# Row maxima of attention: the negated maxima reach row 96 of the query tile by DMA between SBUF tiles

## The reference, cut to what matters

```python
def attend(q, keys, vals, scale):
    s = jnp.einsum('bqhgd,bkhd->bhgqk', q, keys) * scale
    p = jax.nn.softmax(s.astype(jnp.float32), axis=-1).astype(vals.dtype)
    return jnp.einsum('bhgqk,bkhe->bqhge', p, vals)
...
    keys = jnp.concatenate([k_c, k], axis=1)
    vals = jnp.concatenate([v_c, v], axis=1)
```

## Time and profile before

| what | value |
|---|---|
| time, median of 3 runs | 1147.48 us (1145.49 to 1149.68) |
| span of the profiled execution (it has no time of its own beside it) | 1146.1 us |
| TensorE matmuls busy | 1072.0 us, 94% of the span |
| VectorE, ScalarE, GpSimd busy | 440.2, 368.3 and 127.5 us |
| mean granted clock of TensorE | 0.974 |
| heads of layer 0, first to last score product | about 363 to 583 us |
| heads of layer 1 | about 914 to 1088 us |

### The profile page before, as it was taken

How to read it: one execution, slowest core, us unless ns; L and a number is a source line. 1 busy time by engine, 2 the same in 40 slices (tenths; PEclk the granted TensorE clock), 3 DMA queues, 4 the chain that set the end, 5 groups by cost and what they waited for, 6 DMA issues and landing times.

```text
span 1146.1 us, 11426 instructions
## 1 busy us (share of the span) xinstructions
PE 1072.0 (94%) x4139; PEld 610.6 (53%) x4139; DVE 440.2 (38%) x797; ACT 368.3 (32%) x690; POOL 127.5 (11%) x148
## 2 busy tenths in 40 slices
PE   2799999999999999999899899999998999999996
PEld 0455555655455544455568655555444544445474
DVE  1342103312473433554453433122237444454453
ACT  3322113100113344566650332112001234455712
POOL 2000000000242001000440200000003300100530
PEclk8899999999999999999999899999998899999998
DMA  9801012201200222122022411120222000003021
GB/s 351 288 1 56 2 54 74 74 19 56 74 1 1 74 74 77 71 74 74 1 111 69 145 51 55 55 73 1 74 75 73 1 1 1 0 29 119 1 93 73
DMA packets 50965, 74.29 MB, mean 65 GB/s; under 512 B 7812, under 2 KB 30688, under 8 KB 50784
## 3 DMA queue, kind: packets, MB, share of 16 engines
q1 hardware_dynamic: 47088, 60.81, 15.8%
q0 software_dynamic: 3824, 12.77, 3.0%
HBM read 69.37 MB, written 4.19 MB: 64 GB/s over the span
## 4 chain that ended last, share of the span: by engine, by line
PE 86%; DVE 4%; issue 3%; ACT 3%; DMA 2%; POOL 1%; SPq 1%; ACTq 0%; POOLq 0%; DVEq 0%
PE bank L1329 30%; PE pv L1497 10%; PE bank L1548 6%; PE bank L1320 5%; PE bank L1457 3%; PE bank L1579 3%; PE bank L1581 3%; PE bank L1580 3%; PE bank L1435 3%; PE bank L1466 3%; PE bank L1425 2%; DMA W<-in_w_mod 2%; PE bank L1273 2%; PE bank L1405 2%; PE bank L1474 2%
## 5 line engine op out<-in xcount | busy, mean ns | idle before, releaser
L1329 PE MATMUL bank<-hA,W 128*128 128x512 f32 (+1 forms) x992 | 348.3, 510 | 2.7 <-DVE hA L882 1.5
L1329 PEld LDWEIGHTS bank<-hA,W 128*128 128x128 f32 x992 | 187.8, 190 | 154.3 <-issue 142.4
L771 ACT ACTIVATE hA<-bank 128x512 f32<-128x512 f32 (+1 forms) x168 | 93.1, 563 | 91.9 <-PE bank L1548 64.0
L1127 DVE TENSOR_REDUCE mxp<-bank 128x1 f32<-128x384 f32 x192 | 96.5, 551 | 51.0 <-PE bank L1457 50.8
L1497 PE MATMUL pv<-hA,vg 128*128 128x512 f32 (+1 forms) x168 | 85.1, 588 | 6.7 <-ACT hA L771 6.4
L1497 PE MATMUL pv<-hA,XA 128*128 128x512 f32 (+1 forms) x168 | 82.1, 570 | 1.5 <-ACT hA L771 1.5
L1548 PE MATMUL bank<-hA 97*128 97x512 f32 (+1 forms) x168 | 78.1, 565 | 0.0
L1145 DVE SCALAR_TENSOR_TENSOR hA<-pv,hA 64x512 f32<-64x512 f32 (+1 forms) x36 | 21.6, 600 | 113.5 <-ACT hA L714 113.3
L1320 PE MATMUL bank<-W,hA 128*128 128x384 f32 x192 | 63.7, 486 | 0.0
L1580 PE MATMUL bank<-W_parts,hA_parts 128*128 128x512 f32 x160 | 62.3, 389 | 0.0
L911 DVE SCALAR_TENSOR_TENSOR YA<-tz,bank 128x512 f32<-128x512 f32 (+1 forms) x24 | 14.4, 599 | 108.3 <-ACT tz L573 108.3
(11 more groups left out here) (209 smaller groups left out, 1467.9 us busy)
## 6 DMA issues: line engine op xcount, KB each, us to landing
W<-in_w_mod SPq DMA_DIRECT2D x12, 2048.0 KB, 8.0
W<-in_w_in SPq DMA_DIRECT2D x6, 1536.0 KB, 8.5
W<-in_w_in SPq DMA_DIRECT2D x8, 1024.0 KB, 6.1
W<-in_w_out SPq DMA_DIRECT2D x4, 2048.0 KB, 7.8
W<-in_w_in SPq DMA_DIRECT2D x8, 512.0 KB, 4.3
XA<-in_x SPq DMA_DIRECT2D x4, 512.0 KB, 10.9
XA<-in_x POOLq DMA_DIRECT2D x4, 512.0 KB, 7.4
x_between_layers<-XA POOLq DMA_DIRECT2D x4, 512.0 KB, 2.9
```

The lines of the kernel that those rows point to most:

```text
L771: act.activation(prob[slot % 4][:, 0:nq], ps("sc", l, h, q0, kt)[:, 0:nq], ACT.Exp, scale=MLA_SCALE if h < MLA_H else GQA_SCALE)\
L1127: dve.tensor_reduce(mxp[:, t, half:half + 1], ps("mx", l, h, q0, t, half)[:, 0:384], AX, ALU.max).then_inc(*up("part_max", l, h, q0, t, half))
L1329: mm = pe.matmul(p[:, 0:c[1]], w[:, k, s * P:s * P + P], hT[:, k, c[0]:sum(c)], start=(k == 0), stop=(k == KD - 1))
```

## The change

The products of `max_rows` and the copies of `neg_max` are gone. SP moves each column of `nmx` into its 128 columns of row 96 by a DMA: for each head 6 DMAs of 128 words in layer 0 and 4 in layer 1, all from one queue, after the wait for `neg_max`. SP's stream is reordered for this: the first two blocks after the `w_in` blocks are issued ahead of head 0's rows, the others one by one behind the rows of the heads that carry modulation. TensorE waits for all rows of a head (`nm_row`) before its first unit. `MAX_FROM` goes from (3, 2) to (2, 1), so the next head's maxima products start a unit earlier; the new `MOD_AT` keeps the modulation in its units. VectorE's wait before a column of `nmx` is written again now names the rows of head h - 2.

```diff
--- before.py
+++ after.py
@@ -83,7 +83,8 @@
         **{f"z{i}": (4 + i // 4, i % 4) for i in range(8)}}
 LAST_OF = ["ckv0", "gq2", "glak", "tok5", "z3", "z7"]
 RING = 6
-MAX_FROM = (3, 2)
+MAX_FROM = (2, 1)
+MOD_AT = (1, 0)
 
 
 def chunks_of(name, layer):
@@ -358,8 +359,30 @@
             for i in range(1, 4):
                 block_dma(i)
             sp.dma_start(con[:, P:C_END], a["consts"][:, P:C_END]).then_inc(*dma("con_in"))
-            for i in range(4, len(W_SEQ)):
-                block_dma(i)
+
+            def neg_max_row(l, h):
+
+                sp.wait_ge(*at("neg_max", l, h))
+                if h >= 2:
+                    sp.wait_ge(*at("filled", "sc", l, h - 2, 256, TILES - 1))
+                lat, b = lat_of(l), h % 2
+                row = qh[b][96:97, lat] if h < MLA_H else q_high[b][96:97, lat].bitcast(F32)
+                for t in range(TILES - lat.start // P):
+                    with nc.allow_non_contiguous_dma("one word of each partition"):
+                        sp.dma_start(row[:, P * t:P * t + P], nmx[:, b, lat.start // P + t:lat.start // P + t + 1])\
+                            .then_inc(*dma("nm_row", l, h))
+
+            for l in range(DEPTH):
+                for b in range(6):
+                    block_dma(W_POS[("in", l, b)])
+                turns = [h for h in heads if mod_of_head(l, h)]
+                after = W_POS[("in", l, 5)] + 1
+                for i in range(2):
+                    block_dma(after + i)
+                for h in heads:
+                    neg_max_row(l, h)
+                    if h in turns:
+                        block_dma(after + 2 + turns.index(h))
 
 
         @block.gpsimd
@@ -738,21 +761,12 @@
                         act.activation(y_hi[:, k, lat_of(l)], Y[:, k, lat_of(l)], ACT.Copy)\
                             .then_inc(*up("y_hi", l, k))
 
-                def neg_max(h):
-                    for q0, nq, nk in qbs(l):
-                        act.wait_ge(*at("filled", "nm", l, h, q0))
-                        queries = (qh if h < MLA_H else q_high)[h % 2]
-                        act.activation(queries[96:97, q0:q0 + nq], ps("nm", l, h, q0)[96:97, 0:nq], ACT.Copy)\
-                            .then_inc(*up("nm_row", l, h, q0))
-                        let_go(("nm", l, h, q0), "nm_row", l, h, q0)
-
                 head_in(0)
                 round_q(0)
                 for t in out_tiles(l):
                     o_out(t)
                 slot = 0
                 recips = [] if l == 0 else [(0, heads[-1], 256)]
-                neg_max(0)
                 for h in heads:
                     todo = [(q0, nq, kt) for q0, nq, nk in qbs(l) for kt in range(nk // P)]
                     more = h + 1 < len(heads)
@@ -780,9 +794,9 @@
                         if j < 2 and more and h + 1 >= MLA_H:
                             gqa_in(h + 1, j + 1)
                         m = mod_of_head(l, h)
-                        if m and m[2] < 4 and j == MAX_FROM[l] - 2:
+                        if m and m[2] < 4 and j == MOD_AT[l]:
                             mod_rows(*m[1:])
-                        if m and m[2] >= 4 and j == MAX_FROM[l] + 1:
+                        if m and m[2] >= 4 and j == MOD_AT[l] + 3:
 
                             act.wait_ge(*at("filled", "vp", l, TILES - 1))
                             act.wait_ge(*at("filled", "kp", l, MLA_H - 1, LAT))
@@ -799,8 +813,6 @@
                             w_high(2 * c // KD, (2 * c % KD, 2 * c % KD + 1))
                         if j == 3 and len(qbs(l)) == 2:
                             recip(h, *qbs(l)[0][:2])
-                    if more:
-                        neg_max(h + 1)
 
                 y_high((2, 3))
                 recip(heads[-1], *qbs(l)[-1][:2])
@@ -1109,9 +1121,9 @@
 
                 def maxima(h):
                     if h >= 2:
-                        dve.wait_ge(*at("filled", "nm", l, h - 2, 256))
+                        dve.wait_ge(*at("nm_row", l, h - 2))
                     elif l:
-                        dve.wait_ge(*at("filled", "nm", l - 1, 10 + h, 256))
+                        dve.wait_ge(*at("nm_row", l - 1, 10 + h))
                     for q0, nq, nk in qbs(l):
                         for t in range(q0 // P, (q0 + nq) // P):
                             if q0 == 0:
@@ -1457,16 +1469,6 @@
                         close(pe.matmul(p[:, 0:n], q[:, t * P:t * P + P], k[:, n * half:n * half + n],
                                         start=True, stop=True), "mx", l, h, q0, t, half)
 
-                def max_rows(h):
-                    pe.wait_ge(*at("neg_max", l, h))
-                    for q0, nq, nk in qbs(l):
-                        p = open_("nm", l, h, q0)
-                        for j in range(nq // P):
-                            t = q0 // P + j
-                            mm = pe.matmul(p[96:97, P * j:P * j + P], nmx[:, h % 2, t:t + 1], ident, start=True,
-                                           stop=True)
-                        close(mm, "nm", l, h, q0)
-
                 def values(tiles):
                     for t in tiles:
                         p = open_("vp", l, t)
@@ -1528,14 +1530,13 @@
                     else:
                         groups = []
                     flush(1)
-                    max_rows(h)
                     if h + 1 < len(heads):
                         project_k(h + 1)
                     flush(0)
                     units = [(q0, nq, kt, nk // P) for q0, nq, nk in qbs(l) for kt in range(nk // P)]
                     for j, (q0, nq, kt, nkt) in enumerate(units):
                         if kt == 0:
-                            pe.wait_ge(*at("nm_row", l, h, q0))
+                            pe.wait_ge(*at("nm_row", l, h))
                             pe.wait_ge(*at("kh_ones", l, 1))
                             if h >= MLA_H:
                                 pe.wait_ge(*at("q_both", l, h))
@@ -1558,9 +1559,9 @@
                         slot[0] += 1
 
                         m = mod_of_head(l, h)
-                        if m and j == MAX_FROM[l] - 2:
+                        if m and j == MOD_AT[l]:
                             mod(*m[1:])
-                        if m and j == MAX_FROM[l] + (-1 if m[2] < 4 else 1):
+                        if m and j == MOD_AT[l] + (1 if m[2] < 4 else 3):
                             mod_turn(*m[1:])
                         flush(2)
                         if j >= MAX_FROM[l]:
```

## The result

The changed kernel takes 1194.13 us (median of 4 runs, 1191.21 to 1194.83) and the kernel before 1147.59 us in its 4 runs on the same chip. The ratio is 1.0405, with a 95% interval of 1.0385 to 1.0424: the change costs 46.5 us. The direction was forecast; the size was not. 1194 us lies outside the range, beyond every rival.

What follows compares the result with a forecast made beforehand. TensorE, with 86% of the last-ending chain, was taken to set the heads' pace. Terms -11.8 + 5.7 + 11.5 + 9.6 + 2 = +17 us on 1147.5 us gave 1164 us (rounded down), range 1142 to 1184 us.

Steps and rivals of the forecast that it cites:

- The removed work: Boundaries into MLA heads 0 to 4: removed products count in full, 5 x 1.40 + 5 x 0.96 = 11.8 us saved.
- In layer 0 ... nothing there waits: MLA heads, layer 0: context units and modulation product stand ahead, so the earlier maxima products cause no wait.
- each such head grows by 1.72 us: Layer 1 MLA heads: early maxima products wait for rounded queries; +5.2 us for heads 1 to 3, +0.5 in head 0.
- L: Time from the end of the negated maxima to the row in the query tile: 4.3 us layer 0, 3.5 layer 1.
- The clock: TensorE's granted clock falls after new stalls: +2 us in all, bounds 0 and 24 us.
- Most of the slow stretch falls where the head waits for ScalarE anyway: Reason given for putting the lower TensorE clock after stalls at only +2 us in all.
- Rival 3: TensorE's clock falls after most stalls, half of the 24 us counts: 1174 us; chance 0.15.
- The boundaries: Into heads 5 to 11 the row transfer is exposed: +11.5 us in layer 0, +9.6 us in layer 1.
- The sign that was set: TensorE waits 2 us or more for a DMA before first scores of heads 5 to 11, nothing in heads 0 to 4.
- The 19.3 us of the earlier trace: TensorE's idle time before the removed products, 28 parts: at some head boundaries the maxima already arrive late.
- The modulation heads: Heads 7 and 8: gate matmuls wait for a bank; +3.4 and +3.2 us in layer 0, +1.25 twice in layer 1.
- SP's queue at no cost: Weight blocks issued after a head's rows are needed a head or more later: no cost unless a load is late.

Runs made afterwards that it cites:

- e5: Changed kernel with row DMAs only for heads 0 to 4, matmuls and copies for 5 to 11, old maxima start; 1134.78 us, ratio 0.9881.
- e1: Kernel before with only the earlier maxima products (MAX_FROM 2, 1), modulation in its units, columns turned by matmul; 1184.66 us, ratio 1.0343.
- e2: Changed kernel with the old maxima start (MAX_FROM 3, 2) and one added ScalarE wait, so transfers alone; 1184.38 us, ratio 1.0329.
- e6: e2 with dead products on TensorE before the row wait of heads 5 to 11, four in layer 0, three in layer 1; 1171.69 us, ratio 1.0210.
- e4: Changed kernel with dead products before the row wait of heads 5 to 11, three in layer 0, two in layer 1; 1189.53 us, ratio 1.0382.
- e8: e1 with heads 7 and 8 starting the next head's maxima products at the old unit; 1179.78 us, ratio 1.0283.
- e9: e2 with every second row issued by ScalarE's queue instead of SP's; 1170.05 us, ratio 1.0190.

## Why the prediction was right in direction and wrong in size

**The removed work (term of -11.8 us): right.** e5 keeps this term alone and gains about 13 us, with MLA periods shorter by 1.4 and 1.0 us. The rows are hidden there in the changed kernel too. Layer 0, into head 2 (compare):

```profile
401.14 0.16 DVE L1143 TENSOR_REDUCE nmx<-mxp 128x4 f32<-128x8 f32 x1
401.32 3.69 SPq L372 DMA_DIRECT2D hA<-nmx  x6
...
408.99 1.03 PE L1549 MATMUL bank<-hA 97*128 97x256 f32 x4
```

By the 3.69 us of the issues and the 2.0 us of the last landing the row lies at about 406.5, and the scores start at 408.99, without a wait.

**"In layer 0 ... nothing there waits" and "each such head grows by 1.72 us": wrong.** The prediction looked at what a maxima product reads (the rounded queries, the keys) and only in the GQA heads at the bank it writes. In layer 0 the early start costs the MLA heads 0.9 us each (e1), with a wait for the bank in each. In layer 1 the wait for the rounding was sized well (1.63 to 1.75 us), and where the clock holds a head does grow by 1.8 us; but in the changed kernel the clock falls behind all four of these waits, so a head costs 3.4 us and not 1.72. Over the MLA stretches of both layers the forecast had about -5.6 + 4 x (1.72 - 0.96) = -2.6 us, and 7.8 us were measured: 10.4 us more, 3.7 of them in layer 0 and 6.6 from the slow stretches in layer 1.

**L: mis-sized.** 4.3 and 3.5 us were taken, 5.2 and 3.9 us measured; the first is above the upper bound of 5.1, and that bound was built on slow words, which are cheap (8.6 ns). The issue took 0.60 us where the earlier trace rows gave 0.36. The landing of 2.0 us was put at 1.7. The trace of the kernel before did hold packets of 4 bytes, 904 of them on SP's queue, with a mean of 9.6 ns, which would have settled the upper bound. Over seven boundaries a layer that is 7 x 0.9 + 7 x 0.4 = 9.1 us. The half microsecond added for waking the engines is not there: in e2's chain SP issues 0.02 us after the maxima and TensorE starts 0.04 us after the landing. The Trainium skill, "DMA: Bandwidth & Descriptors", section "Anatomy of one DMA — SWDGE (gpsimd) path", puts the fixed part of a DMA issued by GpSimd at about 2.0 us; this trace's 2.0 us from issue to landing on SP's queue agrees.

**The clock (+2 us, bounds 0 to 24): far too low.** With L it is the largest miss that the runs can assign. e6 shows at least 12.7 us where the transfers stand alone. In the changed kernel the slow stretches behind the rounding cost 6.6 us, and e4's GQA stretches get 4.1 us back by a better clock, which makes 10.7 us or more; the most that the clock can have cost the GQA stretches is 24 us. The prediction's reason, "Most of the slow stretch falls where the head waits for ScalarE anyway", may hold in part there: of some 16 us of missing clock that e4 gives back, 4.1 shorten the stretches. It does not hold in layer 1's MLA heads, where TensorE leads the chain and the prediction counted no slow stretch. Rival 3 named this cause, though for the stalls of the rows; its 10 us were nearer.

**The boundaries.** From first score to first score, by the boundary at the end of it (us more than before):

| into head | 5 | 6 | 7 | 8 | 9 | 10 | 11 |
|---|---|---|---|---|---|---|---|
| layer 0, forecast | 0 | 2.5 | 1.8 | 3.4 | 3.2 | 1.2 | -0.6 |
| layer 0, measured | 1.9 | 3.9 | 2.9 | 4.8 | 6.2 | 2.2 | 3.8 |
| layer 1, forecast | 1.85 | 1.8 | 1.4 | 1.25 | 1.25 | 0.9 | 1.1 |
| layer 1, measured | 3.6 | 5.2 | 2.7 | 1.3 | 2.3 | 1.7 | 2.2 |

Into head 10 of layer 0, which was worked out from rows, the mechanism came as told: the first exponential 0.7 us after the first score, VectorE's first reduce 6.4 us after it. L is 0.9 us of the 1.0 that is missing. The boundaries that were only likened to it, each trusted to 1 us, are off by up to 4.4 us. The sign that was set, a wait of 2 us or more for the DMA, came at all seven boundaries of layer 0 and at one of layer 1. The 19.3 us of the earlier trace rows, read as maxima that arrive late already, count the idle time of weight loads too: TensorE's matmuls waited there 3.8 us in 14 waits, none over 0.3.

**The modulation heads: right in kind, too small.** The broadcast waits for VectorE's first reduce, 1.37 us in e1. Forecast were +3.4 and +3.2 us for heads 7 and 8 of layer 0 with L in it, and +4.8 and +6.2 came; e8 takes back 3.2 and 1.5 us of the part that is the early start's.

**SP's queue at no cost: right** as far as the profile goes. TensorE waits 9.7 us for weight blocks of `w_mod`, 8.7 before and 8.5 in e2, which has the changed kernel's order on SP; and e2's chain runs through the issues of the rows alone.

**Together.** The span grew by 46.9 us against +17, 29.9 more. The MLA stretches hold 10.4 of that (7.8 for -2.6). The GQA stretches hold 18.7: 37.5 measured, where the terms into heads 5 to 10, without the 1.85 that stands in the MLA stretch already, come to about 18.8. The row's way explains 7.8 of it (6 x 0.9 + 6 x 0.4; the boundary into 11 lies outside the stretch), and 10.9 are left for the clock, the banks and the keys of head 6. At least 4.1 of them are the clock's (e4); how the rest divides stays open. The last 0.8 us lie outside the four stretches.

## What to carry to other kernels

Before a product is moved earlier, look at three waits: for what it reads, for the bank it writes, and for what then stands behind it; the work moved is not late alone, but holds up the queue. Price a small DMA on the critical path as the number of serial issues times one issue, plus one landing, and hide it behind work that is already there: in e5 the transfers gain about 13 us in all, where 6.0 and 5.1 us of work cover ways of 5.2 and 3.9, and in e2 they lose where 0.6 us does. A stall of TensorE should be priced as the stall and the slow stretch that may follow, as far as TensorE leads the chain there: full price in e1's layer 1, part of it in e4.

## What the runs showed of the hardware

- An issue on SP's queue of 128 single words to one row of an SBUF tile takes 0.60 us (0.47 for the first of a burst), where a plain load of 128 rows took 0.36. The queue takes the next after 0.04 us.
- Two queues issue at the same time, but landing slows from 2.0 to 2.5 and 2.9 us (e9, rows of heads 6 to 11).
- A 4-byte packet between SBUF tiles costs its DMA engine 8.6 ns (e9).
- The granted clock can fall after a stall of 1.4 to 1.6 us (0.64 over the 4 us behind the wait of 1.63 us in the changed kernel), but did not after the 1.67 us of the earlier trace rows, where it was 1.00 from 1000 to 1008 us. In e1 it fell behind one wait of 1.75 us and held behind the next but one of the same length. It fell to the lower level in e2's stall of 4.6 us into head 9 and stayed up at e6's of 1.1 us there. Four dead products (3.60 us in the trace) ahead of such a wait made e2 faster by 12.7 us.
